# Tiled TensorE modes in a hybrid decoder step: heads alternated in scores, values and state products, samples' expert values in four column groups

## The reference

```python
def token_mix(xn, ...):
    proj = xn @ w_in                       # q, k, v, z, x/B/C, dt
    q, k = apply_partial_rope(q), apply_partial_rope(k)
    attn = rmsnorm(attend(q, k, v), g_attn)      # 16 heads of 64, causal, softmax
    xbc, conv_new = causal_conv(xbc, ...)
    y, ssm_new = ssd_scan(xs, dt, a, b_in, c_in, ssm_state)   # 16 heads of 64, chunks of 128, state 128
    y = _rms_by_group((y + d_skip * xs) * silu(z)) * g_ssd
    return concat([attn, y]) @ w_out, k, v, conv_new, ssm_new

def peer_ffn(xn, wq, sub_keys, u_emb, v_emb):    # 128 x 128 experts, 8 heads, top 16
    e, g = product_key_top16(xn @ wq, sub_keys)
    act = gelu(einsum('cd,chkd->chk', xb, u_emb[e]), approximate=False)
    return einsum('chk,chkd->cd', g * act, v_emb[e])

h = x + token_mix(rmsnorm(x)); h = h + peer_ffn(rmsnorm(h)); y = rmsnorm(h)
```

## Time and profile before

| | |
|---|---|
| median of 3 runs | 1233.85 us (1231.4 to 1236.24) |
| the profiled execution | 1229.45 us, its span 1227.3 us |
| PE busy | 1199.8 us, 98% of the span |
| POOL busy | 753.8 us, 61% |
| DVE busy | 785.8 us, 64% |
| ACT busy | 571.5 us, 47% |
| HBM traffic | 182 GB/s over the span |
| mean granted clock of TensorE | 0.996 |

### The profile page before, as it was taken

The page is one execution under the profiler, slowest core; times in us unless marked ns, Lnnn a source line. Parts: engine busy times, 40 slices in busy tenths (PEclk is TensorE's granted clock), DMA queues, the critical chain, the costliest instruction groups (busy, mean ns, idle before and its releaser), DMA issues.

```text
span 1227.3 us, 23601 instructions
## 1 busy us (share of the span) xinstructions
PE 1199.8 (98%) x7463; PEld 1039.8 (85%) x7463; DVE 785.8 (64%) x1749; ACT 571.5 (47%) x1287; POOL 753.8 (61%) x622
## 2 busy tenths in 40 slices
PE   7999999999999999999999999999999999999997
PEld 5877888745988899999999999998888888888766
DVE  4579787666139999400599999994544555666334
ACT  3222323252435555556555554444555555555435
POOL 0058241003835599998776767666776798798645
PEclk9999999999999999999999999999999999999999
DMA  6565575287645276666544444444665697788523
GB/s 210 164 214 148 166 257 155 88 288 272 184 150 156 88 224 190 188 186 182 162 141 144 142 142 140 145 140 145 189 189 188 188 325 259 238 282 269 184 97 111
DMA packets 99863, 224.88 MB, mean 183 GB/s; under 512 B 11682, under 2 KB 12306, under 8 KB 99274
## 3 DMA queue, kind: packets, MB, share of 16 engines
q1 hardware_dynamic: 96762, 214.52, 56.2%
q0 software_dynamic: 2304, 8.39, 2.0%
q10 hardware_dynamic: 720, 1.01, 0.2%
HBM read 215.61 MB, written 8.19 MB: 182 GB/s over the span
## 4 chain that ended last, share of the span: by engine, by line
PE 68%; issue 1%; POOL 1%; DVE 0%; ACT 0%; DVEq 0%; POOLq 0%; ACTq 0%
PE bank L1551 29%; PE bank L1521 28%; PE bank L1531 5%; PE bank L1474 2%; PE bank L1486 1%; PE bank L1582 1%; PE bank L1498 1%; POOL hl L1399 1%; PE bank L1571 0%; POOL hl L1414 0%; DVE acts L1941 0%; ACT acts L1751 0%; PE bank L1600 0%; PE bank L1564 0%; DVEq L1319 0%
## 5 line engine op out<-in xcount | busy, mean ns | idle before, releaser
L1399 POOL TENSOR_TENSOR hl<-ring,hl 128x512 fp32r<-128x512 f32 x448 | 586.1, 1319 | 195.1 <-ACT hl L1631 186.2
L1631 ACT CAST hl<-ring 128x512 fp32r<-128x512 f32 x512 | 316.8, 620 | 301.0 <-PE bank L1551 168.0
L1521 PE MATMUL bank<-split,hl 128*128 128x256 f32 x3072 | 378.7, 282 | 0.5 <-ACT hl L1631 0.3
L1521 PEld LDWEIGHTS bank<-split,hl 128*128 128x128 f32 x3072 | 366.3, 188 | 1.2 <-POOL hl L1399 0.6
L1551 PE MATMUL bank<-hl,split 128*128 128x512 f32 x1524 | 353.6, 394 | 0.0
L1551 PEld LDWEIGHTS bank<-hl,split 128*128 128x128 f32 x1524 | 285.9, 188 | 67.8 <-issue 0.9
L481 PE MATMUL pj<-xn,ring 128*128 128x264 f32 x704 | 165.0, 390 | 1.4 <-DMA ring<-in_w_ring 1.4
L1911 DVE TENSOR_TENSOR split<-acts,split 128x256 fp32r<-128x256 f32 x128 | 128.1, 1022 | 50.3 <-ACT split L1727 46.5
L481 PEld LDWEIGHTS pj<-xn,ring 128*128 128x128 f32 x704 | 132.3, 192 | 25.7 <-issue 2.8
L1918 DVE TENSOR_TENSOR hl<-ring,hl 128x512 fp32r<-128x512 f32 x64 | 45.1, 705 | 119.8 <-ACT hl L1631 119.8
L457 POOL TENSOR_TENSOR wo<-ring,wo 128x512 fp32r<-128x512 f32 x32 | 46.9, 1473 | 95.5 <-ACT wo L856 95.4
(11 more groups left out here) (339 smaller groups left out, 1218.4 us busy)
## 6 DMA issues: line engine op xcount, KB each, us to landing
ring<-in_uv SPq DMA_DIRECT2D x256, 256.0 KB, 2.7
ring<-in_v_rows SPq DMA_DIRECT2D x256, 256.0 KB, 3.1
ring<-in_w_ring SPq DMA_DIRECT2D x76, 512.0 KB, 3.7
room<-in_cache_k SPq DMA_DIRECT2D x16, 512.0 KB, 5.3
room<-in_cache_v SPq DMA_DIRECT2D x16, 512.0 KB, 4.7
hs<-in_state_ssm SPq DMA_DIRECT2D x8, 512.0 KB, 4.7
out_ssm_s<-hs SPq DMA_DIRECT2D x8, 512.0 KB, 5.8
acts<-x_rows SPq DMA_DIRECT2D x8, 512.0 KB, 5.5
```

What stands on the lines that cost most here:

```text
L1399: nc.gpsimd.tensor_tensor(hl[:, r % HL, 1], raw[:, r], hl[:, r % HL, 0].bitcast(F32), ALU.subtract).then_inc(lo_done, 1)
L1521: mm = nc.tensor.matmul(out, hl[:, r % HL, m, k * P:(k + 1) * P], split[:, x, kk, 0:TP], start=(kk == 0 and n == 0), stop=(kk == KD - 1 an ...
L1631: nc.scalar.copy(hl[:, r % HL, 0], raw[:, r]).then_inc(hi_done, 1)
```

## The change

Three products of the head pairs and the samples' sum are written anew, with the same arithmetic on the values that are kept.

- `scores`: both transposes first, then the 128-column products of head 0 and head 1, then their 256-column products. Each product still uses the 64 rows of its head.
- `attend` and `mixed`: the weights of a product are now the 64 columns of its head, and the output goes to that head's 64 partitions; the two heads alternate product by product.
- `samples`: four groups of output partitions (0, 32, 64, 96) take two samples each. `wz[:, b]` has two columns, the residual is 32 products of two weight columns instead of 8 of eight. DVE clears the two banks first (`smp_zero`) and writes the weights with two instructions. Norm and scaling go over 128 partitions, and the samples' outputs are stored by 8 DMAs instead of 2.

In the built program the products carry a tile of TensorE's array: 64 x 128 (rows x columns) at row 0 or 64 in `scores`, before and after; 128 x 128 before and 128 x 64 at column 0 or 64 after in `attend` and `mixed`; 128 x 32 at column 0 before, and at 0, 32, 64, 96 after in `samples`. The cached pages' products stay as they were.

```diff
@@ scores
                     for j in range(2):
-                        r = slice(j * HD, (j + 1) * HD)
                         nc.tensor.transpose(hd[j][:, 3 * P:4 * P], proj[:, V0 + c, j * P:(j + 1) * P], ident)
-                        nc.tensor.matmul(hd[j][:, 0:P], proj[r, Q0 + c, 0:P], proj[r, K0 + c, 0:P], start=True, stop=True)
-                        nc.tensor.matmul(hd[j][:, P:3 * P], proj[r, Q0 + c, P:TP], proj[r, K0 + c, 0:TP], start=True, stop=True
-                                         ).then_inc(s_ready, 1)
+                    for q0, q1, k1, at in ((0, P, P, 0), (P, TP, TP, P)):
+                        for j in range(2):
+                            r = slice(j * HD, (j + 1) * HD)
+                            mm = nc.tensor.matmul(hd[j][:, at:at + k1], proj[r, Q0 + c, q0:q1], proj[r, K0 + c, 0:k1], start=True, stop=True)
+                            if q0:
+                                mm.then_inc(s_ready, 1)
@@ attend
-                    for j in range(2):
-                        pe.wait_ge(pt_copied, 2 * c + j + 1)
-                        nc.tensor.matmul(hd[j][:, 0:P], vtok[:, 0], pt[:, j, 0:P], start=True, stop=True)
-                        nc.tensor.matmul(hd[j][:, P:TP], vtok[:, 0], pt[:, j, P:2 * P], start=True, stop=False)
-                        nc.tensor.matmul(hd[j][:, P:TP], vtok[:, 1], pt[:, j, 2 * P:3 * P], start=False, stop=True
-                                         ).then_inc(o_ready, 1)
+                    for n, (k, at) in enumerate(((0, 0), (0, P), (1, P))):
+                        for j in range(2):
+                            r = slice(j * HD, (j + 1) * HD)
+                            if n == 0:
+                                pe.wait_ge(pt_copied, 2 * c + j + 1)
+                            mm = nc.tensor.matmul(hd[j][r, at:at + P], vtok[:, k, r], pt[:, j, n * P:(n + 1) * P],
+                                                  start=(n < 2), stop=(n != 1))
+                            if n == 2:
+                                mm.then_inc(o_ready, 1)
@@ mixed
-                    for j in range(2):
-                        at = j * TP
-                        nc.tensor.matmul(yb[:, at:at + P], xtok[:, 0], wgt[:, j, 0:P], start=True, stop=True)
-                        nc.tensor.matmul(yb[:, at + P:at + TP], xtok[:, 1], wgt[:, j, P:TP], start=True, stop=False)
-                        mm = nc.tensor.matmul(yb[:, at + P:at + TP], h0[:], cs[:, j], start=False, stop=True)
+                    for n, k in enumerate((0, 1, 1)):
+                        for j in range(2):
+                            r, at = slice(j * HD, (j + 1) * HD), j * TP + k * P
+                            mm = nc.tensor.matmul(yb[r, at:at + P], h0[:, r] if n == 2 else xtok[:, k, r],
+                                                  cs[:, j] if n == 2 else wgt[:, j, k * P:(k + 1) * P], start=(n < 2), stop=(n != 1))
@@ samples
-                        pe.wait_ge(gelu_done, NKEY)
-                        residual(smp, NB, TP)
-                        pe.wait_ge(wz_done, 1)
-                        for b in range(NB):
-                            pe.wait_ge(rows_in[b], 32)
+                        pe.wait_ge(smp_zero, 2)
+                        for k in range(KD):
+                            for j in range(SIDE):
+                                nc.tensor.matmul(smp[k // 4][j * SPAN:j * SPAN + NQ, k % 4 * P:(k % 4 + 1) * P], res[:, k, TP + j:NT:SIDE], ident,
+                                                 start=(k % 4 == 0), stop=False)
+                        pe.wait_ge(wz_done, 2)
+                        for q in range(NQ):
                             for half in range(2):
-                                mm = nc.tensor.matmul(smp[half][0:NB], wz[:, b], rows8[:, b, half * (D // 2):(half + 1) * (D // 2)],
-                                                      start=False, stop=(b == NB - 1))
+                                for j in range(SIDE):
+                                    b = q * SIDE + j
+                                    if half == 0:
+                                        pe.wait_ge(rows_in[b], 32)
+                                    mm = nc.tensor.matmul(smp[half][j * SPAN:j * SPAN + NQ], wz[:, b],
+                                                          rows8[:, b, half * (D // 2):(half + 1) * (D // 2)], start=False, stop=(q == NQ - 1))
@@ DVE, after group 24
+                        if g == GD + NB:
+                            dve.wait_ge(gelu_done, NKEY)
+                            for bank_s in smp:
+                                nc.vector.memset(bank_s[:], 0.0).then_inc(smp_zero, 1)
```

More of the change, by code:

```diff
@@ L51 @@
 HS, NS = 4, 6
+SIDE, SPAN = 4, 32
+NQ = NB // SIDE
 N_IN, N_OUT, N_Q = PROJ, KD * MIXC // KD, 2 * PH
@@ L1244, in build @@
             hdot = sb("hdot", [P, 2, NB], where=s8)
-            wz = sb("wz", [P, NB, NB], where=s8)
+            wz = sb("wz", [P, NB, NQ], where=s8)
             ss = sb("ss", [P, TILES, 2], where=s8)
@@ L1385, in _ @@
                     for n in range(2 * TT + 2):
-                        k, half = (TT, n) if n < 2 else ((n - 2) // 2, n % 2)
-                        rows = NB if k == TT else P
+                        half = n % 2
+                        cols = slice(half * (D // 2), (half + 1) * (D // 2))
                         sp.wait_ge(y_done, n + 1)
-                        store(sp, t["y_out"][k * P:k * P + rows, half * (D // 2):(half + 1) * (D // 2)],
-                              y10[0:rows, k, half * (D // 2):(half + 1) * (D // 2)])
+                        if n < 2:
+                            for j in range(SIDE):
+                                store(sp, t["y_out"][TP + j:NT:SIDE, cols], y10[j * SPAN:j * SPAN + NQ, TT, cols])
+                        else:
+                            k = (n - 2) // 2
+                            store(sp, t["y_out"][k * P:(k + 1) * P, cols], y10[:, k, cols])
                     sp.wait_ge(out_done, 16 * outs[0])
@@ L1574, in samples @@
                     def samples():
-                        pe.wait_ge(gelu_done, NKEY)
-                        residual(smp, NB, TP)
-                        pe.wait_ge(wz_done, 1)
-                        for b in range(NB):
-                            pe.wait_ge(rows_in[b], 32)
-                            for half in range(2):
-                                mm = nc.tensor.matmul(smp[half][0:NB], wz[:, b], rows8[:, b, half * (D // 2):(half + 1) * (D // 2)],
-                                                      start=False, stop=(b == NB - 1))
+                        pe.wait_ge(smp_zero, 2)
[5 more added lines that the diff above has]
+                        for q in range(NQ):
+                            for half in range(2):
+                                for j in range(SIDE):
+                                    b = q * SIDE + j
[3 more added lines that the diff above has]
+                                                          rows8[:, b, half * (D // 2):(half + 1) * (D // 2)], start=False, stop=(q == NQ - 1))
                         mm.then_inc(smp_done, 1)
@@ L1739, in _ @@
                             for half in range(2):
-                                nc.scalar.activation(sqd[0:NB, half * (D // 2):(half + 1) * (D // 2)], smp[half][0:NB], ACT.Square,
-                                                     accum_out=ss[0:NB, TT, half:half + 1]).then_inc(sq10, 1)
+                                nc.scalar.activation(sqd[:, half * (D // 2):(half + 1) * (D // 2)], smp[half][:], ACT.Square,
+                                                     accum_out=ss[:, TT, half:half + 1]).then_inc(sq10, 1)
                         if g == GX + 2:
                             act.wait_ge(var10, 1)
-                            nc.scalar.activation(rs10[0:NB, TT:TT + 1], rs10[0:NB, TT:TT + 1], ACT.Sqrt).then_inc(root10, 1)
+                            nc.scalar.activation(rs10[:, TT:TT + 1], rs10[:, TT:TT + 1], ACT.Sqrt).then_inc(root10, 1)
                         if g == GD + NB:
@@ L1959, in _ @@
                         if g == GX + 1:
-                            norm(TT, NB, 2)
+                            norm(TT, P, 2)
                         if g == GX + 2:
-                            scale(TT, NB, 1, smp)
+                            scale(TT, P, 1, smp)
+                        if g == GD + NB:
+                            dve.wait_ge(gelu_done, NKEY)
+                            for bank_s in smp:
+                                nc.vector.memset(bank_s[:], 0.0).then_inc(smp_zero, 1)
                         if g == GD + NB + 1:
@@ L1965, in _ @@
                             dve.wait_ge(wz_zero, 1)
-                            nc.vector.tensor_tensor(wz[:].rearrange("p a b -> p (a b)")[:, ::NB + 1], hdot[:, 1], ig[:, 2, TP:NT], ALU.mult
-                                                    ).then_inc(wz_done, 1)
+                            for q in range(NQ):
+                                b = slice(q * SIDE, (q + 1) * SIDE)
```

(2 more changed lines are left out.)

1 line of the change is left out of this document (added).

## The result

The changed kernel takes 1210.46 us (median of 4 runs, 1209.94 to 1214.61) against 1233.92 us before (median of 4 runs; the table further up has three of them). The ratio is 0.983, 95% interval 0.9809 to 0.985: 1.7% faster. I had forecast 1224 us with a range from 1213 to 1241. The direction was right, the gain more than twice what I had forecast, and the time lies outside the range. The profiled execution took 1214.61 us (its span 1212.5), the slowest of the four; what its trace shows of that is told at the end.

What follows compares the result with a forecast made beforehand. TensorE, busy for 98% of the span, was taken to bound the kernel. The loop's -5.7 us and the samples' -4.7 us, together -10.3 us, took 1233.85 us to 1223.5, say 1224 us, range 1213 to 1241.

Steps and rivals of the forecast that it cites:

- What bounds, and what a pass costs: TensorE, busy 98% of the span, bounds the kernel; passes of 128, 256, 512 columns cost 0.11, 0.216, 0.432 us.
- Hardly at all elsewhere: TensorE's waits: 3.1 and 1.3 us for probabilities, transposed and plain, in the eight turns, hardly any in other places.
- n alternated products of two passes take n + 1 slots: `mixed`, `attend`, `scores`, `samples`: partial overlap, n + 1 slots instead of 2n; chance of this main case 0.57.
- -4.7: `samples`: residual +1.9 us and values -6.5 us, together -4.7 us, counted in full.
- changes of division: Loop turns: switching how the array is divided costs 0.185 us each, six a turn instead of four, +0.37 us.
- The +10 us for loads: Loop: 24 passes a turn on 64 weight columns would each wait half of 0.11 us for a load; not used.
- Rival 2: Loop and `samples`: parts overlap fully, four at once in `samples`; sum -18.7 us, 1215 us; chance 0.08.
- -0.33 us a turn: Loop under Rival 2: 6 slots instead of 7 and 128-column scores in half the time, -2.6 us in all.
- The savings in `scores` ... are lost in the wait: Turns 1 to 5: a circle through DVE and ACT sets the pace; only `attend` and `mixed` gain, -2.8 us.
- What was costed at nothing: `samples`: DVE's two clears (1.4 us if uncovered), second `wz` product, norm and scaling, six more stores (under 1 us).
- 5.7 + 2.6 = 8.3 us: Loop: the main case's sum of -5.7 us with Rival 2's further -2.6 us.

Runs made afterwards that it cites:

- e4: The changed kernel with all products of one column group in `samples` in a row before the next group's: 1219.3 us.
- e5: The changed kernel with two products (four passes) of a column group in a row in `samples` before the next group's: 1210.6 us, one run.
- e11: The changed kernel with four products (eight passes) of a column group in a row in the residual, values alternated product by product: 1210.93 us, one run.
- e2: The changed kernel with `scores`, `attend` and `mixed` as before, so only the samples' part of the change: 1220.86 us.
- e8: The changed kernel with v's two transposes moved from the head of `scores` to behind `attend`: 1210.11 us.
- e6: The changed kernel with two column groups of four samples in `samples` instead of four groups: 1214.62 us, one run.
- e9: The changed kernel with `attend` moved behind the turn's last tile, directly ahead of `mixed`, v's transposes ahead of it: 1209.65 us.
- e10: The changed kernel run once more, unaltered, on the same chip as e9: 1212.97 us against 1229.23 us for the kernel before.

## Why the prediction was wrong

1. **What bounds, and what a pass costs: right.** A pass that went on TensorE shortened the kernel in both places, the experiments took nothing back after the loop, and the price of a pass (0.11, 0.216, 0.432 us) is the length of a slot now. Two waits were passed over. "Hardly at all elsewhere" leaves out 5.3 and 3.5 us ahead of the turns and 2.8 us behind them, where nothing changed; and the wait in turn 1 for L1058, 0.63 us, had no term and is 1.19 us now.
2. **"n alternated products of two passes take n + 1 slots": this step failed.** I let passes start in program order, so that a product's second pass held back the next head's first. The records show the first passes of both heads 6 ns apart and of all four groups within 21 ns. Two parts need n slots and four parts n/2. e4, e5 and e11 show what happens in its place: three passes can wait for a busy part while the next part starts, so one waiting second pass holds nothing back. In `samples` this turned -4.7 into -10.3 us; in `scores` the 128-column products overlap too (the eight passes take four slots, 2 x 0.11 + 2 x 0.216 = 0.65 us, and 0.85 us to the tile with what the changes of division add), though I had priced them at nothing because of their wide weights. Loads of 128 columns for the two row halves also start in pairs, 7 ns apart. The +10 us for loads that cannot run beside a pass on the same rows, which I set aside, did not come either: with weights of 64 columns the slot is 0.109 us.
3. **Rival 2, full overlap, was the case that happened,** and 1215 us its price; I gave it 0.08 because of "the two passes of a product in a row". That was an argument and no row. Between ends with no row near either, 0.08 was too little. Its price was also put together wrongly: -0.33 us a turn leaves out that the 256-column products would take two slots instead of three, and is counted in all eight turns, though in turns 1 to 5 I held the scores' savings for lost. Both heads side by side throughout give -1.31 us for turn 0 (6 slots less in `mixed`, 2 of 0.11 and 2 of 0.216 us less in `scores`); measured are -1.37.
4. **"The savings in `scores` ... are lost in the wait": right in turns 3 and 4, wrong in others, and for a reason that I did not have.** I moved head 0's scores later by their old length. They came earlier, and the masks end 0.4 us sooner after the release. In turns 3 and 4 DVE's slower decay instructions beside GpSimd take that back before ACT's copy; in turns 2 and 5 the copy comes 0.56 and 0.77 us earlier. Turns 1 to 5 gained 5.3 us against the trace of before and 4.3 us against e2's, instead of 2.8. Two terms were mis-sized within them: `attend` gains 0.26 us there, not 0.56, since head 1's six slots begin only after its own copy, 0.38 us behind head 0's, and from `mixed` to DVE's release it is 0.61 us, not 0.56. Turn 0 gained 1.4 us instead of 0.8.
5. **The changes of division: right.** Six a turn, at 0.15 to 0.2 us each, against 0.185 in the prediction. Removing one (e8) was worth 0.2 us in turn 7 and nothing in paced turns.
6. **What was costed at nothing cost nothing:** `samples` waited for no clear, and the rest of the last stage is 51.31 us against 51.33.

With full overlap the loop would have been 5.7 + 2.6 = 8.3 us by the prediction's own sum, and the whole 18.7 us; measured in the traces are 9.6 and 19.9. Part of that agreement is luck, by item 3, and the loop is only 8.7 us shorter than e2's, whose code in it is that of before.

## What to carry over

Small products on TensorE that use half or a quarter of its rows or output partitions are worth putting on different parts of the array side by side: here they took a half and a quarter of the time, in fp32. Keep runs for one part short, at most four passes (two fp32 products), and gather neighbours with the same division, since each change costs 0.15 to 0.2 us. Where the two inputs become ready one after the other, side by side gains less: 0.26 us instead of 0.54 in `attend` here. Then look at who takes the results: where another engine paces the loop, what counts is when it gets its input, not TensorE's busy time, and an earlier start can be lost again beside a third engine.

## What the runs showed of the hardware

- Passes on different parts of the array run together in fp32 at the full rate: 32 passes of 512 columns in 3.55 us on four column groups, 6.96 us on two (e6), 13.83 us on one. The Trainium skill ("TensorE: Matmul & The Clock Gate", Part 3) has 3.07 times for four row tiles; here, on four column groups, the values gained 3.9 times. The same section has matmuls start in program order. Here they do not: in e5 group 1's second pass stands ahead of group 2's first in the program, and starts 0.1 us after it.
- Three passes can wait for a busy part before the ones behind are held up (group 2 starts beside the 13th of 16 passes in e4, beside the fifth of 8 in e11, and within 40 ns with all others in e5).
- A DVE instruction took nearly three times as long beside one of GpSimd: the decay instructions of 128x128 took 0.75 to 0.77 us while `hs<-hs,up` ran and 0.27 us after it.
- The granted clock moves the time by itself. In the profiled execution of the changed kernel it fell to its lower level, 1.2 GHz, at 71.2 and at 272.6 us, where it stayed at 2.4 GHz in the trace of before, and it was low for 6.8 us instead of 3.4 at 348 us. In stretches around the first two (columns: stretch, its length, PE, PEld, DVE, ACT, POOL busy, then PEclk, DMA share, GB/s):

```profile
71.00:75.00 4.00, 4.00 (x11) 3.12 (x12) 1.71 (x7) 0.76 (x2) 0.00 (x0) 0.57 0.38 155
272.00:277.00 5.00, 5.00 (x15) 2.89 (x15) 0.36 (x2) 0.00 (x0) 0.00 (x0) 0.66 0.57 218
```

TensorE was busy throughout both, but not with the same work ahead of them. Before the first it had waited 2.12 us for weights, until 70.86; before, the same wait was 1.35 us long and the clock stayed up. The second began while TensorE ran 24 small passes (L631 with 16 columns, L656 with 8), with no idle time from 262 us on. It also stands in the traces of e2, e4, e9 and e10, each time within 1.2 us of this block's end, and is missing in the others, which have the same block. While the clock is low a pass of the tile at 71 us takes 0.44 us instead of 0.22. The stretch from the key pages to the output projection took 63.83 us in this execution, and 61.72 to 62.45 us in most of the traces without the second fall (63.44 in e1). This goes with the mean granted clock of 0.991, against 0.995 in the three executions of 1209.94 to 1210.57 us. That the falls make up most of the difference is my estimate, since those three have no trace. Why the clock falls in some executions and not in others is open.
